# Attention in a hybrid layer: large probability tiles scaled in two halves, and rope and VectorE's query units one tile step later

## The chip, the core and the metric

The kernel runs on one core of a Trainium2 chip. The metric is device time in microseconds of one execution; lower is better. The core has five engines with queues of their own: TensorE (PE, with its weight loads shown apart as PEld), VectorE (DVE), ScalarE (ACT), GpSimd (POOL) and SyncE (SP), which issues the transfers. Each engine runs its instructions strictly in the order in which they were written, and engines meet only at semaphores: `wait_ge` holds an engine's queue until a counter has reached a value.

## The reference, cut to what matters

The program is one decoder layer: half a SwiGLU feed-forward block, a token mixer of two branches (latent attention and a gated recurrence), and another half feed-forward block. The change touches the attention alone, 206 of 2229 us:

```python
q = (_rmsnorm(c_q, q_norm_g) @ w_uq).reshape(b, s, MLA_HEADS, QK_NOPE + QK_ROPE)
kv = (_rmsnorm(c_kv, kv_norm_g) @ w_ukv).reshape(b, s, MLA_HEADS, QK_NOPE + V_HEAD)
...
q_rope = _apply_rope(q_rope, cos[:, :, None, :], sin[:, :, None, :])
...
sc = jnp.einsum('bqhd,bkhd->bhqk', qn, k_nope) + jnp.einsum('bqhr,bkr->bhqk', qr, k_rope)
sc = jnp.where(causal[None, None], sc * scale, -jnp.inf)
p = jax.nn.softmax(sc, axis=-1).astype(v.dtype)
return jnp.einsum('bhqk,bkhd->bqhd', p, v)
```

There are 1024 positions, 8 heads, and per head 64 plain and 32 rotary dimensions for queries and keys and 64 for values, all in float32.

## The kernel before

**Numbers.** Every float32 operand of a product is split into a high and a low part; a product of two split operands is three matmuls (lines 88 to 90). ScalarE writes the high part (line 94) and VectorE the low part (line 98), so each operand passes ACT and then DVE.

**Tiles.** Attention goes through 64 tiles, n = 8h + s: head h, block s of 128 queries. A tile of block s sees s + 1 blocks of 128 keys, so it has 128 to 1024 columns. Tiles with s of 4 and above have more than 512 columns, and two pieces (b = 0, the first 512 columns, and b = 1, the rest); smaller tiles have one. Below, a head with even number is E, with odd number O, and "O4" is its tile of block 4.

**Path of one tile.** PE computes the scores (`scores`, L88 to L90 with tiles a_k and a_q, closed by the mask matmul L2245). DVE takes the negated row maximum (L2256). ACT takes the exponential with the row sum (`exponent`, L2266). POOL raises the sum to the power -1 (L2272) and scales the probabilities by it (L2275). PE transposes each block of 128 columns (`turn`, L2290) into PSUM banks 4 (piece 0) and 5 (piece 1). ACT and DVE split the transposed pieces (`turned_hi`, `turned_lo`, tile a_pt, L94 and L98). Twice per head PE multiplies them with the values (`product`, L2322), and ACT and DVE take the output (a_o, L2338 and L2343).

**Steps.** Each engine runs a function of its own for each step n, in this order (the step's function names are in the code below):

- PE: [product at s = 3 and 7], scores of n, transposes of n - 2, [the projection of a unit].
- DVE: [output], maximum of n, low parts of n - 2, [low part of rope], [low part of a pair of heads], [unit].
- ACT: [output], high parts of n - 2, [rope], exponential of n, [unit].
- POOL: [rope], normalisation of n.

**Units.** The queries and keys of the next head are projected in between, in units of 512 positions: a unit is 9 matmuls on PE for a query half ("q") and 6 for a key half ("k", for two heads at once). `beside(n)` says which unit runs beside tile n: in even heads q half 0 at s = 1 and q half 1 at s = 7; in odd heads k half 0 at s = 1, q half 0 at s = 3, k half 1 at s = 6, q half 1 at s = 7. The last head has none, so 14 query units run beside tiles. All write PSUM bank 7, so PE's next unit waits until DVE has done with the one before (`u_dve`). For a query unit ACT copies the plain rows (L2163), and DVE multiplies the rotary rows by sine and cosine (L2188, L2189, into the single buffers a_rot and a_rot2) and writes the low part of the plain rows (L2191). "Rope" is what follows: POOL adds the two products (L2207), ACT writes the high part (L2175), DVE the low part (L2216).

**Waits around the change.** `turn` of tile n needs tile n's scaled probabilities (`norm_done`) and, since the banks are shared, the low parts of the same piece of tile n - 1 (`pt_split`). `scores` of n needs the exponential of n - 2 (`p_done`).

Of the kernel before, what the change touches and what calls it, by code (L numbers as in the profile page):

```python
# [19 lines left out]
ALU = mybir.AluOpType  # L20
# [3 lines left out]
P = 128  # L24
# [4 lines left out]
HALF = 512  # L29
# [34 lines left out]
class Core:  # L64


    def __init__(self, nc, ctx):
        self.nc, self.ctx = nc, ctx
        self.ps = ctx.enter_context(nc.psum_tensor("ps", [P, 8, HALF], F32))
        self.squared = None  # L70
# [30 lines left out]
def half_of(hf):  # L101
    return slice(hf * HALF, (hf + 1) * HALF)
# [134 lines left out]
class TileNorm:  # L237
# [118 lines left out]
    def turn(self, pe, t, b, bank_free=None):  # L356
        pe.wait_ge(self.S["gained_r"], self.pres + t + 1)
        if bank_free is not None:
            pe.wait_ge(self.S["u_split"], self.split_count(bank_free))
        for k in range(DK):  # L360
            last = pe.transpose(self.c.ps[:, b + k // 4, (k % 4) * P:(k % 4 + 1) * P],  # L361
                                self.work(t)[:, k * P:(k + 1) * P], self.c.ident[:, :])
        last.then_inc(self.S["turned"], 1)
# [1612 lines left out]
HEAD_TILES = NT  # L1976
# [3 lines left out]
class Attention:  # L1980
# [6 lines left out]
    def __init__(self, c, w, lat, w_uq, w_ukv):  # L1987
        self.c, self.nc, self.w, self.lat = c, c.nc, w, lat
        names = ("v_done", "v_hi", "v_lo", "zero", "kr_hi", "kr_split", "kr_copied", "unit_done", "q_hi", "q_rot", "q_sum", "rope_hi", "q_split",
                 "k_hi", "u_dve", "s_done", "max_done", "p_done", "norm_done", "t_done", "pt_hi", "pt_split", "o_done",  # L1990
                 "o_aux", "o_add", "o_hi", "o_split")
        self.S = {n: c.sem("a_" + n) for n in names}
        vq = w_uq.rearrange("(k p) (h e) -> p k h e", p=P, h=HEADS)
        vkv = w_ukv.rearrange("(k p) (h e) -> p k h e", p=P, h=HEADS)
        self.n_v = w.new(KC * HEADS * VH)
        for k in range(KC):
            w.piece(self.n_v, w.raw_of(self.n_v)[:, k * HALF:(k + 1) * HALF].rearrange("p (h e) -> p h e", e=VH),
                    vkv[:, k, :, NOPE:NOPE + VH])
        self.n_a = []
        half = ROPE // 2  # L2000
        for h in range(HEADS):
            n = w.new(QC * P + (0 if h % 2 else KC * P))
            q = w.raw_of(n)[:, 0:QC * P].rearrange("p (k f) -> p k f", f=P)
            even = ((0, QK, 0), (QK, half, NOPE + half), (QK + half, half, NOPE))
            odd = ((0, half, NOPE + half), (half, half, NOPE), (ROPE, ROPE, NOPE), (NOPE, NOPE, 0))
            for to, width, at in odd if h % 2 else even:
                w.piece(n, q[:, :, to:to + width], vq[:, :, h, at:at + width])
            if h % 2 == 0:
                for k in range(KC):
                    w.piece(n, w.raw_of(n)[:, (QC + k) * P:(QC + k + 1) * P].rearrange("p (h e) -> p h e", e=NOPE),  # L2010
                            vkv[:, k, h:h + 2, 0:NOPE])
            self.n_a.append(n)
        u = AT_U
        self.pt_hi, self.pt_lo = (c.at(u + 16384 * i, f"a_pt{i}", [P, 8, 4, P], F32R) for i in range(2))
        self.q_hi, self.q_lo = ([c.at(u + 32768 + 4096 * (2 * par + i), f"a_q{par}{i}", [P, SEQ], F32R) for par in range(2)]
                                for i in range(2))
        k_at = (u + 49152, u + 57344, AT_AREA + 73728)
        self.k_hi, self.k_lo = ([c.at(at + 4096 * i, f"a_k{n}{i}", [P, SEQ], F32R) for n, at in enumerate(k_at)] for i in range(2))
        self.v = c.at(AT_AREA + 40960, "a_v", [P, HEADS, NT, P], F32R)
        self.rot, self.rot2 = c.at(AT_AREA + 81920, "a_rot", [P, HALF]), c.at(AT_AREA + 100352, "a_rot2", [P, HALF])  # L2020
        self.probs = c.at(AT_AREA + 83968, "a_probs", [P, 3, SEQ])
        self.o = c.at(AT_AREA + 96256, "a_o", [P, SEQ])
        self.o_lo3 = c.at(AT_AREA + 36864, "a_o_lo3", [P, SEQ], F32R)
        self.neg, self.rs, self.inv = (c.at(BASE + 2400 + 64 * i, f"a_s{i}", [P, 16]) for i in range(3))
        self.scale = float(QK) ** -0.5

        self.units = [("q", 0, 0), ("k", 0, 0), ("q", 0, 1), ("k", 0, 1)]
        for h in range(HEADS - 1):
            if h % 2:
                self.units += [("k", (h + 1) // 2, 0), ("q", h + 1, 0), ("k", (h + 1) // 2, 1), ("q", h + 1, 1)]  # L2030
            else:
                self.units += [("q", h + 1, 0), ("q", h + 1, 1)]
        self.index = {unit: i for i, unit in enumerate(self.units)}
        self.closes = [self.index[("k", 0, 1)]] + [self.index[("q", h, 1)] for h in range(1, HEADS)]
# [234 lines left out]
    def normalise(self, pool, n):  # L2269
        i = n % 16  # L2270
        pool.wait_ge(self.S["p_done"], n + 1)
        self.nc.gpsimd.tensor_tensor(self.inv[:, i:i + 1], self.rs[:, i:i + 1], self.c.expo[:, 1:2], ALU.pow)\  # L2272
            .then_inc(self.S["norm_done"], 1)
        pool.wait_ge(self.S["norm_done"], 2 * n + 1)
        self.nc.gpsimd.tensor_scalar(self.prob(n), self.prob(n), self.inv[:, i:i + 1], 1.0, ALU.mult, ALU.mult)\  # L2275
            .then_inc(self.S["norm_done"], 1)

    def turn(self, pe, n):
        c, s = self.c, n % HEAD_TILES
        pe.wait_ge(self.S["norm_done"], 2 * n + 2)  # L2280
        if n == 0:
            pe.wait_ge(self.S["u_dve"], 4)
        for b in self.pieces(n):
            if b == 0 and n > 0:
                pe.wait_ge(self.S["pt_split"], self.piece(n - 1, 0) + 1)
            if b == 1 and n >= HEAD_TILES or b == 1 and s > 4:
                pe.wait_ge(self.S["pt_split"], self.piece(n - 1 if s > 4 else n - 5, 1) + 1)
            for j in range(4 * b, min(4 * b + 4, s + 1)):
                at = s - j if b else j
                last = pe.transpose(c.ps[:, 4 + b, at * P:(at + 1) * P], self.prob(n)[:, j * P:(j + 1) * P], c.ident[:, :])  # L2290
            last.then_inc(self.S["t_done"], 1)
# [69 lines left out]
    def act_step(self, act, n):  # L2361
        h, s = n // HEAD_TILES, n % HEAD_TILES
        if s == 7:
            self.take(act, h, 0)
        if s == 3 and h > 0:
            self.take(act, h - 1, 1)
        if n >= 2:
            self.turned_hi(act, n - 2)
        if s == 3 and h > 0 and h % 2 == 0:
            self.pair_hi(act, h // 2 - 1, slice(0, SEQ), 2 * h)  # L2370
        if n == HEADS * HEAD_TILES - 1:
            self.pair_hi(act, 3, half_of(0), 2 * HEADS - 1)
        if n < HEADS * HEAD_TILES:
            if n > 0 and self.beside(n - 1):
                self.rope_act(act, self.beside(n - 1))
            self.exponent(act, n)
            if self.beside(n):
                self.unit_act(act, self.beside(n))

    def dve_step(self, dve, n):  # L2380
        h, s = n // HEAD_TILES, n % HEAD_TILES
        if s == 7:
            self.add(dve, h, 0)
        if s == 3 and h > 0:
            self.add(dve, h - 1, 1)
        if n < HEADS * HEAD_TILES:
            self.maximum(dve, n)
        if n >= 2:
            self.turned_lo(dve, n - 2)
        if n < HEADS * HEAD_TILES:  # L2390
            if n > 0 and self.beside(n - 1):
                self.rope_dve(dve, self.beside(n - 1))
            if s == 3 and h > 0 and h % 2 == 0:
                self.pair_lo(dve, h // 2 - 1, slice(0, SEQ), h // 2)
            if n == HEADS * HEAD_TILES - 1:
                self.pair_lo(dve, 3, half_of(0), 4)
            if self.beside(n):
                self.unit_dve(dve, self.beside(n))

    def pool_step(self, pool, n):  # L2400
        if n > 0 and self.beside(n - 1):
            pool.wait_ge(self.S["norm_done"], 2 * n)
            self.rope_pool(pool, self.beside(n - 1))
        self.normalise(pool, n)

    def pe_step(self, pe, n):
        h, s = n // HEAD_TILES, n % HEAD_TILES
# [237 lines left out]
def hybrid_layer(nc, a, out):  # L2645
# [6 lines left out]
    with ExitStack() as ctx:  # L2652
# [47 lines left out]
        with nc.Block() as block:  # L2700
# [530 lines left out]
            def _(pe):  # L3231
# [8 lines left out]
                for q in range(NT):  # L3240
                    turn(f1, q)
# [123 lines left out]
```

## Time and profile before

| what | us |
|---|---|
| median of 3 runs (2231.65 to 2235.87) | 2233.1 |
| the profiled execution, its own time | 2231.14 |
| span of its profile | 2229.3 |
| attention's tile steps in the profile | about 1237 to 1443 |
| one pair of heads within them (1304.44 to 1355.20) | 50.76 |

The span is the time between the first and last recorded instruction. In the profile's rows, start times are microseconds from the span's start; a bracket gives the idle time of the engine ahead of an instruction and the instruction that released it. Matmuls are pipelined, so the busy times of successive ones overlap.

### The profile page before, as it was taken

What the parts mean: (1) busy time and instruction counts of PE and PEld (TensorE: products, weight loads), DVE (VectorE), ACT (ScalarE), POOL (GpSimd) and SP (SyncE); (2) the same over time, 40 slices, a digit from 0 to 9 for tenths busy, and PEclk for the clock granted to TensorE, in tenths of its full rate; (3) what the DMA queues carried; (4) which work ended last, traced back from release to release, by engine and by line L of the source; (5) the groups of instructions that cost most, each with busy time, mean ns of one, the idle gap of its engine ahead of it and who ended that gap; (6) DMA issues with size and microseconds to landing.
All of it is one profiled execution on the core that took longest, in us unless ns stands there. A gap on an engine that the chain in (4) does not pass through costs nothing.

```text
span 2229.3 us, 25934 instructions
## 1 busy us (share of the span) xinstructions
PE 2145.4 (96%) x9837; PEld 1780.6 (80%) x9837; DVE 1367.7 (61%) x1719; ACT 979.3 (44%) x1559; POOL 405.3 (18%) x444
## 2 busy tenths in 40 slices
PE   5999999999999999999999888899899999999998
PEld 4888788878887888888888677788788888888886
DVE  7667865557587656211212788677856766557666
ACT  6443333334364776311323666545533333333444
POOL 3123320000032221000011455402213331000012
PEclk9999999999999999999999999999999999999999
DMA  3355442253442111222410100265335453216234
GB/s 123 95 171 186 159 166 71 68 196 102 153 161 84 52 52 50 76 67 66 134 43 25 29 10 10 104 218 194 108 103 190 165 193 119 71 51 228 94 137 156
DMA packets 220293, 249.85 MB, mean 112 GB/s; under 512 B 24261, under 2 KB 161546, under 8 KB 220170
## 3 DMA queue, kind: packets, MB, share of 16 engines
q1 hardware_dynamic: 220170, 248.19, 34.0%
q8 instruction: 79, 1.29, 0.2%
q14 instruction: 44, 0.36, 0.0%
HBM read 192.06 MB, written 55.57 MB: 111 GB/s over the span
## 4 chain that ended last, share of the span: by engine, by line
PE 86%; DVE 6%; ACT 3%; issue 2%; POOL 2%; DMA 0%; SPq 0%; POOLq 0%; ACTq 0%; DVEq 0%
PE ps L88 28%; PE ps L90 28%; PE ps L89 28%; PE ps L2322 1%; PE ps L2290 1%; ACT a_probs L2266 1%; POOL a_rot L2207 1%; DVE a_pt L98 1%; PE ps L361 0%; DVE a_s L2256 0%; DVE w_lo L98 0%; DVE entry_y L346 0%; DVE exit_x L1337 0%; DMA entry_x<-in_x_dram 0%; DVE ff_w_lo L98 0%
## 5 line engine op out<-in xcount | busy, mean ns | idle before, releaser
L98 DVE TENSOR_TENSOR ff_w_lo<-ff_raw,ff_w_hi 128x512 fp32r<-128x512 f32 x264 | 214.0, 814 | 171.8 <-ACT ff_w_hi L94 171.5
L88 PE MATMUL ps<-ff_t,ff_w_hi 128*128 128x512 f32 x704 | 274.1, 389 | 0.4 <-DVE ff_w_lo L98 0.2
L90 PE MATMUL ps<-ff_t,ff_w_lo 128*128 128x512 f32 x704 | 273.9, 389 | 0.0
L89 PE MATMUL ps<-ff_t,ff_w_hi 128*128 128x512 f32 x704 | 273.9, 389 | 0.0
L94 ACT ACTIVATE ff_w_hi<-ff_raw 128x512 fp32r<-128x512 f32 x264 | 164.9, 627 | 179.5 <-PE ps L90 173.0
L88 PE MATMUL ps<-d_b_hi,d_a_hi 128*128 128x512 f32 x608 | 237.5, 391 | 3.8 <-DVE d_a_lo L98 3.7
L90 PE MATMUL ps<-d_b_hi,d_a_lo 128*128 128x512 f32 x608 | 236.6, 389 | 0.0
L89 PE MATMUL ps<-d_b_lo,d_a_hi 128*128 128x512 f32 x608 | 236.6, 389 | 0.0
L98 DVE TENSOR_TENSOR w_lo<-w_raw,w_hi 128x1024 fp32r<-128x1024 f32 (+2 forms) x81 | 90.5, 1119 | 233.2 <-ACT w_hi L94 233.2
L88 PE MATMUL ps<-ff_b,ff_w_hi 128*128 128x512 f32 x528 | 208.0, 394 | 6.0 <-ACT ff_u2x L696 5.0
L89 PE MATMUL ps<-ff_b,ff_w_hi 128*128 128x512 f32 x528 | 206.8, 392 | 0.0
L90 PE MATMUL ps<-ff_b,ff_w_lo 128*128 128x512 f32 x528 | 206.7, 391 | 0.0
L88 PE MATMUL ps<-u_hi,w_hi 128*128 128x512 f32 x512 | 199.7, 390 | 0.0
L90 PE MATMUL ps<-u_hi,w_lo 128*128 128x512 f32 x512 | 199.4, 389 | 0.0
L89 PE MATMUL ps<-u_lo,w_hi 128*128 128x512 f32 x512 | 199.3, 389 | 0.0
L88 PEld LDWEIGHTS ps<-ff_t,ff_w_hi 128*128 128x128 f32 x704 | 132.1, 188 | 28.7 <-DVE ff_w_lo L98 0.6
L89 PEld LDWEIGHTS ps<-ff_t,ff_w_hi 128*128 128x128 f32 x704 | 132.1, 188 | 27.5
L90 PEld LDWEIGHTS ps<-ff_t,ff_w_lo 128*128 128x128 f32 x704 | 132.1, 188 | 27.3
L94 ACT ACTIVATE w_hi<-w_raw 128x1024 fp32r<-128x1024 f32 (+2 forms) x81 | 78.3, 968 | 151.7 <-PE ps L90 145.2
L88 PEld LDWEIGHTS ps<-d_b_hi,d_a_hi 128*128 128x128 f32 x608 | 114.1, 188 | 29.5 <-DVE d_a_lo L98 6.1
L90 PEld LDWEIGHTS ps<-d_b_hi,d_a_lo 128*128 128x128 f32 x608 | 114.1, 188 | 23.6
L89 PEld LDWEIGHTS ps<-d_b_lo,d_a_hi 128*128 128x128 f32 x608 | 114.2, 188 | 23.5
(301 smaller groups left out, 4297.6 us busy)
## 6 DMA issues: line engine op xcount, KB each, us to landing
ff_raw<-in_ffn_w_gate_dram SPq DMA_DIRECT2D x44, 512.0 KB, 3.9
ff_raw<-in_ffn_w_up_dram SPq DMA_DIRECT2D x44, 512.0 KB, 4.0
d_sums<-in_ffn_w_down_dram SPq DMA_DIRECT2D x44, 512.0 KB, 4.1
sums_scratch<-d_sums SPq DMA_DIRECT2D x88, 256.0 KB, 2.6
w_raw<-in_w_in_dram SPq DMA_DIRECT2D x32, 512.0 KB, 4.0
d_raw<-sums_scratch SPq DMA_DIRECT2D x24, 512.0 KB, 3.3
w_raw<-in_w_out_dram SPq DMA_DIRECT2D x24, 512.0 KB, 4.2
spill_scratch<-ff_st SPq DMA_DIRECT2D x44, 256.0 KB, 2.9
```

Of the source, the lines that this page charges most:

```text
L88: pe.matmul(out, lh, rh, start=start, stop=False, skip_group_check=go_on)
L89: pe.matmul(out, lh, rl, start=False, stop=False, skip_group_check=go_on)
L90: return pe.matmul(out, ll, rh, start=False, stop=stop, skip_group_check=go_on)
L94: return nc.scalar.activation(hi, src, ACT.Copy)
L98: return nc.vector.tensor_tensor(lo, src, as_f32(hi), ALU.subtract)
L2207: self.nc.gpsimd.tensor_tensor(self.rot[rope, :], self.rot[rope, :], self.rot2[rope, :], ALU.add)\
L2266: self.nc.scalar.activation(self.prob(n), self.seen(n), ACT.Exp, bias=self.neg[:, i:i + 1], scale=1.0, accum_out=self.rs[:, i:i + 1]).then ...
L2290: last = pe.transpose(c.ps[:, 4 + b, at * P:(at + 1) * P], self.prob(n)[:, j * P:(j + 1) * P], c.ident[:, :])
L2322: last = pe.matmul(c.ps[:, 6, first * P:HALF], self.v[:, h, j, :], pt[:, unit, first:4, :].rearrange("p b q -> p (b q)"), start=j + i == 0 ...
```

## The change

Three things change, all within the tile steps.

1. `normalise` scales a tile of more than 512 columns by one instruction per piece, and each adds one to `norm_done`; the power has a semaphore of its own (`inv_done`). `turn` waits for `norm_done` piece by piece.
2. On DVE, a query unit beside tile n moves from the end of step n to the end of step n + 1. Key units stay. The rope's steps on ACT and DVE move from step n + 1 to n + 2.
3. On POOL, the rope addition of the unit beside n stays in step n + 1, but comes behind tile n + 1's normalisation.

PE's order is the same in both.

```diff
     def normalise(self, pool, n):
...
         self.nc.gpsimd.tensor_tensor(self.inv[:, i:i + 1], self.rs[:, i:i + 1], self.c.expo[:, 1:2], ALU.pow)\
-            .then_inc(self.S["norm_done"], 1)
-        pool.wait_ge(self.S["norm_done"], 2 * n + 1)
-        self.nc.gpsimd.tensor_scalar(self.prob(n), self.prob(n), self.inv[:, i:i + 1], 1.0, ALU.mult, ALU.mult)\
-            .then_inc(self.S["norm_done"], 1)
+            .then_inc(self.S["inv_done"], 1)
+        pool.wait_ge(self.S["inv_done"], n + 1)
+        for b in self.pieces(n):
+            part = self.prob(n)[:, b * HALF:min((b + 1) * HALF, (n % HEAD_TILES + 1) * P)]
+            self.nc.gpsimd.tensor_scalar(part, part, self.inv[:, i:i + 1], 1.0, ALU.mult, ALU.mult).then_inc(self.S["norm_done"], 1)
 
     def turn(self, pe, n):
         c, s = self.c, n % HEAD_TILES
-        pe.wait_ge(self.S["norm_done"], 2 * n + 2)
         if n == 0:
             pe.wait_ge(self.S["u_dve"], 4)
         for b in self.pieces(n):
+            pe.wait_ge(self.S["norm_done"], self.piece(n, b) + 1)
...
     def act_step(self, act, n):
...
-            if n > 0 and self.beside(n - 1):
-                self.rope_act(act, self.beside(n - 1))
+            if n > 1 and self.beside(n - 2):
+                self.rope_act(act, self.beside(n - 2))
             self.exponent(act, n)
...
     def dve_step(self, dve, n):
...
-            if n > 0 and self.beside(n - 1):
-                self.rope_dve(dve, self.beside(n - 1))
+            if n > 1 and self.beside(n - 2):
+                self.rope_dve(dve, self.beside(n - 2))
...
-            if self.beside(n):
+            before = self.beside(n - 1) if n > 0 else None
+            if before and before[0] == "q":
+                self.unit_dve(dve, before)
+            if self.beside(n) and self.beside(n)[0] == "k":
                 self.unit_dve(dve, self.beside(n))
 
     def pool_step(self, pool, n):
+        self.normalise(pool, n)
         if n > 0 and self.beside(n - 1):
-            pool.wait_ge(self.S["norm_done"], 2 * n)
+            pool.wait_ge(self.S["norm_done"], self.piece(n, len(self.pieces(n)) - 1) + 1)
             self.rope_pool(pool, self.beside(n - 1))
-        self.normalise(pool, n)
```

The order on DVE at the passage from an even to an odd head (tiles E7, O0, O1), before, from the low parts of E5 on:

```order
L98 TENSOR_TENSOR a_pt_165<-ps,a_pt_164 128x2x128
L2188 TENSOR_TENSOR a_rot_178<-ps,trig 32x512
L2189 TENSOR_TENSOR a_rot<-ps,trig 32x512
L2191 SCALAR_TENSOR_TENSOR a_q_169<-ps,a_q_167 64x512
L2256 TENSOR_REDUCE a_s_182<-ps 128x1
L98 TENSOR_TENSOR a_pt_165<-ps,a_pt_164 128x4x128
L98 TENSOR_TENSOR a_pt_165<-ps,a_pt_164 128x3x128
L2216 SCALAR_TENSOR_TENSOR a_q_169<-a_rot,a_q_167 32x512
L2256 TENSOR_REDUCE a_s_182<-ps 128x1
L98 TENSOR_TENSOR a_pt_165<-ps,a_pt_164 128x4x128 x2
```

and the same place in the changed kernel:

```order
L98 TENSOR_TENSOR a_pt_165<-ps,a_pt_164 128x2x128
L2256 TENSOR_REDUCE a_s_182<-ps 128x1
L98 TENSOR_TENSOR a_pt_165<-ps,a_pt_164 128x4x128
L98 TENSOR_TENSOR a_pt_165<-ps,a_pt_164 128x3x128
L2188 TENSOR_TENSOR a_rot_178<-ps,trig 32x512
L2189 TENSOR_TENSOR a_rot<-ps,trig 32x512
L2191 SCALAR_TENSOR_TENSOR a_q_169<-ps,a_q_167 64x512
L2256 TENSOR_REDUCE a_s_182<-ps 128x1
L98 TENSOR_TENSOR a_pt_165<-ps,a_pt_164 128x4x128 x2
L2216 SCALAR_TENSOR_TENSOR a_q_169<-a_rot,a_q_167 32x512
```

The unit's three instructions moved behind the maximum of O0 and the low parts of E6, and the rope's low part (L2216) behind the maximum of O1 and the low parts of E7.

The order on POOL from tile O4 to O5, before; the first row is the rope of the query unit beside O3:

```order
L2207 TENSOR_TENSOR a_rot<-a_rot,a_rot_178 32x512
L2272 TENSOR_TENSOR a_s_184<-a_s_183,expo 128x1
L2275 TENSOR_SCALAR a_probs<-a_probs,a_s_184 128x640
L2272 TENSOR_TENSOR a_s_184<-a_s_183,expo 128x1
L2275 TENSOR_SCALAR a_probs<-a_probs,a_s_184 128x768
```

and in the changed kernel:

```order
L2272 TENSOR_TENSOR a_s_184<-a_s_183,expo 128x1
L2277 TENSOR_SCALAR a_probs<-a_probs,a_s_184 128x512
L2277 TENSOR_SCALAR a_probs<-a_probs,a_s_184 128x128
L2207 TENSOR_TENSOR a_rot<-a_rot,a_rot_178 32x512
L2272 TENSOR_TENSOR a_s_184<-a_s_183,expo 128x1
L2277 TENSOR_SCALAR a_probs<-a_probs,a_s_184 128x512
L2277 TENSOR_SCALAR a_probs<-a_probs,a_s_184 128x256
```

The rope's addition moved behind the power and the scaling of O4, and each scaling became two instructions.

## Rows read from the trace of the kernel before

**Rows 1.** The page: busy time of each engine.

```profile
PE 2145.4 (96%) x9837; PEld 1780.6 (80%) x9837; DVE 1367.7 (61%) x1719; ACT 979.3 (44%) x1559; POOL 405.3 (18%) x444
```

**Rows 2.** Windows: length, then busy us of PE, PEld, DVE, ACT, POOL; granted clock.

```profile
1236.00:1442.00 206.00, 177.48 (x998) 147.00 (x997) 162.95 (x258) 135.36 (x294) 104.36 (x142) 0.96 0.13 42
1304.44:1355.20 50.76, 43.84 (x259) 36.44 (x258) 42.59 (x68) 34.83 (x76) 26.87 (x36) 1.00 0.04 11
...
1297.50:1300.90 3.40, 3.40 (x15) 2.99 (x15) 2.67 (x4) 1.78 (x5) 2.19 (x4) 0.50 0.01 2
```

**Rows 3.** Waits in 1236 to 1442: us in total, times, longest us.

```profile
PE ps L2290 <- DVE a_pt L98: 22.5, 20, 1.8
ACT a_q L2175 <- POOL a_rot L2207: 19.9, 14, 1.9
...
PEld ps L2290 <- POOL a_probs L2275: 2.7, 8, 0.7
```

**Rows 4.** Timeline of PE, 1308 to 1340: start us, us, instruction, [idle before].

```profile
1308.95 0.23 PE L2245 MATMUL ps<-mask_b,ident_b 128*128 128x128 bf16 x1
...
1312.17 1.06 PE L2290 MATMUL ps<-ident,a_probs 128*128 128x128 f32 x8 [1.80 <-DVE a_pt L98]
1312.99 0.48 PE L88 MATMUL ps<-ckv,w_hi 128*128 128x512 f32 x1
...
1322.40 0.23 PE L2245 MATMUL ps<-mask_b,ident_b 128*128 128x128 bf16 x1
...
1325.10 0.63 PE L2290 MATMUL ps<-ident,a_probs 128*128 128x128 f32 x4 [1.01 <-DVE a_pt L98]
...
1332.98 0.47 PE L88 MATMUL ps<-cq,w_hi 128*128 128x512 f32 x1
...
1339.23 0.47 PE L88 MATMUL ps<-cq,w_hi 128*128 128x512 f32 x1
```

**Rows 5.** Timeline of DVE, 1308 to 1332.

```profile
1308.87 0.68 DVE L2188 TENSOR_TENSOR a_rot<-ps,trig 32x512 f32<-32x512 f32 x1 [0.41 <-PE ps L90]
...
1311.02 0.29 DVE L2256 TENSOR_REDUCE a_s<-ps 128x1 f32<-128x128 f32 x1
1311.34 1.16 DVE L98 TENSOR_TENSOR a_pt<-ps,a_pt 128x512 fp32r<-128x512 f32 x2
...
1321.63 0.69 DVE L2188 TENSOR_TENSOR a_rot<-ps,trig 32x512 f32<-32x512 f32 x1 [0.57 <-PE ps L90]
...
1325.88 0.96 DVE L2256 TENSOR_REDUCE a_s<-ps 128x1 f32<-128x768 f32 x1
...
1330.70 1.39 DVE L98 TENSOR_TENSOR a_k<-ps,a_k 64x512 fp32r<-64x512 f32 x2 [0.81 <-ACT a_k L94]
```

**Rows 6.** Timeline of ACT, 1309 to 1331.

```profile
1309.66 0.98 ACT L94 ACTIVATE a_pt<-ps 128x512 fp32r<-128x512 f32 x2 [0.20 <-PE ps L2290]
...
1323.00 0.49 ACT L94 ACTIVATE a_pt<-ps 128x384 fp32r<-128x384 f32 x1 [0.77 <-PE ps L2290]
1324.51 0.62 ACT L2175 ACTIVATE a_q<-a_rot 32x512 fp32r<-32x512 f32 x1 [1.02 <-POOL a_rot L2207]
...
1326.87 0.90 ACT L2266 ACTIVATE a_probs<-ps,a_s 128x768 f32<-128x768 f32 x1 [0.34 <-DVE a_s L2256]
```

**Rows 7.** Timeline of POOL, 1308 to 1325.

```profile
1308.85 0.55 POOL L2272 TENSOR_TENSOR a_s<-a_s,expo 128x1 f32<-128x1 f32 x1 [2.04 <-ACT a_probs L2266]
...
1318.85 1.15 POOL L2275 TENSOR_SCALAR a_probs<-a_probs,a_s 128x384 f32<-128x384 f32 x1
...
1323.20 1.28 POOL L2207 TENSOR_TENSOR a_rot<-a_rot,a_rot 32x512 f32<-32x512 f32 x1 [0.23 <-DVE a_rot L2189]
```

**Rows 8.** Groups by shape in 1236 to 1442: busy us, mean ns | idle.

```profile
L2275 POOL TENSOR_SCALAR a_probs<-a_probs,a_s 128x1024 f32<-128x1024 f32 x8 | 9.0, 1124 | 0.8
...
L2275 POOL TENSOR_SCALAR a_probs<-a_probs,a_s 128x512 f32<-128x512 f32 x8 | 5.6, 696 | 0.8
...
L2275 POOL TENSOR_SCALAR a_probs<-a_probs,a_s 128x128 f32<-128x128 f32 x8 | 3.0, 376 | 0.8
```

More of the change, by code:

```diff
@@ L1989, in __init__ @@
         names = ("v_done", "v_hi", "v_lo", "zero", "kr_hi", "kr_split", "kr_copied", "unit_done", "q_hi", "q_rot", "q_sum", "rope_hi", "q_split",
-                 "k_hi", "u_dve", "s_done", "max_done", "p_done", "norm_done", "t_done", "pt_hi", "pt_split", "o_done",
+                 "k_hi", "u_dve", "s_done", "max_done", "p_done", "inv_done", "norm_done", "t_done", "pt_hi", "pt_split", "o_done",
                  "o_aux", "o_add", "o_hi", "o_split")
```

## The prediction, on record before the run

> **What bounds the kernel now.** The page's busy times come first: PE is busy for 2145 of 2229 us [rows 1], so what stands outside attention (matmul on matmul) cannot be touched by this change, which moves nothing there. The windows come next: in attention's 206 us PE is busy for 177.5, so 28.5 us of pauses are all that a better order could win. A pair of heads takes 50.76 us, with PE pausing for 6.9 and DVE for 8.2 [rows 2]. The waits say for what: 22.5 us go to transposes that wait for DVE's low parts of the tile before (`pt_split`), and only 2.7 to transposes that wait for POOL's scaling [rows 3]. So the bound is a chain that passes through PE and DVE in turn: maximum, low parts and units stand in one queue on DVE, and PE waits for some of them. The timeline then shows where: 1.80 us ahead of E7's transposes and 1.01 ahead of O3's [rows 4]. In both places a query unit stands on DVE ahead of the low parts waited for.
>
> **Part 1, scaling in halves.** A scaling has a fixed part: 0.376 us for 128 columns, 0.696 for 512, 1.124 for 1024 [rows 8]. Two halves of 512 take 1.39, so the first is ready 0.43 earlier and the second 0.27 later, and the 32 large tiles cost POOL 32 x 0.27 = 8.6 us more, in a queue that is idle half of the time (104 busy of 206 [rows 2]). What PE can gain is at most the 2.7 us of rows 3, and the part of that which belongs to small tiles stays. I take 0 to -1, and 0 in the sum, because the second half is later, and what is behind it on POOL (the rope, part 3) too.
>
> **Part 2, the query unit on DVE a step later.** A unit is 2.15 us on DVE (1308.87 to 1311.02 [rows 5]). Before, it ran while DVE had nothing else: scores and high parts of the next step were not there yet. Now it stands behind them. I walk through the places with the rows' durations.
>
> *Place A, from an even to an odd head.* PE's unit q1 is done at 1308.87, when DVE starts. The scores of O0 end at 1308.95 + 0.23 = 1309.2 [rows 4], so DVE now waits, does the maximum in 0.3 until 1309.5, and waits again: ACT's high part of E6 starts at 1309.66 and its first piece takes some 0.6 of the 0.98 for both [rows 6]. The low parts take 0.7 and 0.5, until 1311.5 (1.16 for both [rows 5]). E7's transposes can start at 1311.1 instead of 1312.17, a gain of 1.0. But then comes the unit, 1311.5 to 1313.6, and PE's next unit (k half 0) overwrites the bank that it reads. It started at 1312.99 [rows 4] and now starts at about 1313.75: **+0.8**. The pause was moved, not removed, and it grew.
>
> *Place B, tiles O3 to O7.* DVE is free at 1321.63 - 0.57 = 1321.06 [rows 5] and now waits for the scores of O4, until 1322.40 + 0.23 = 1322.6 [rows 4]. The maximum is 0.83 (between 0.29 for one block and 0.96 for six [rows 5]), until 1323.45; the high part of O2 ends at 1323.49 [rows 6], its low part at 1324.0. O3's transposes gain the 1.0 of rows 4. The unit follows until 1326.15, its two rotary products until 1325.45; the maximum of O5 until 1327.1 (before: 1325.88 + 0.96 = 1326.84) and the low part of O3 until 1327.8.
>
> **Part 3, the rope.** In the waits ACT stood 19.9 us for POOL's rope addition [rows 3]; it stood ahead of an exponential. It still does, one tile later. On POOL the addition is now behind O4's normalisation: exponential of O4 from 1323.5 to 1324.4, power 0.55 [rows 7], halves 0.70 and 0.38 [rows 8], with the gaps until 1326.35; the addition 1.28 [rows 7] until 1327.65; ACT's part 0.62 [rows 6] until 1328.3. The exponential of O5 started at 1326.87 [rows 6] and now starts 1.4 later. DVE's low part of rope ends at 1329.0, the maximum of O6 (1.1) at 1330.1. Before, 1326.84 + 0.7 + 1.1 gives 1328.7. The exponential of O6 and the key copies behind it on ACT slip with it, so DVE's key unit moves from 1330.70 [rows 5] to about 1331.9, and PE's q1, which waits for it, from 1332.98 [rows 4] to 1333.45: +0.45.
>
> *Place C, from an odd to an even head.* DVE has the key unit (1.4), the output (0.6), the maximum of O7 (1.2) and the low parts of O5 (1.0) until 1336.15; then the maximum of the next tile. ACT does O7's exponential and the query copy until 1336.9 and the first high piece of O6 until 1337.5. Low parts until 1338.7, unit until 1340.85, PE's next unit at 1341.0 instead of 1339.23 [rows 4]: **+1.8**, with B's 0.45 in it.
>
> *Place D, tiles E1 to E4.* The query unit moves behind the maximum of E2, in a stretch where DVE waited for the rope and for a weight's high part; the rope's low part now stands ahead of the pair's low part. By my walk 0 to +0.3; I take 0.
>
> **Sum.** A pair costs 0.8 + 1.8 = 2.6 by the walk, 2.9 with D. Counted by DVE's pauses instead: 1.5 for 0.41 at A, 1.3 + 0.5 for 0.57 at B, which is 2.3. I take 2.4. There are three pairs (from head 0's E7 to head 6's): 7.2. At the last passage, to head 7, no unit follows on PE, and only the product waits: +0.4. Together **+7.6 us**. The profiled execution took 2231.14, which gives 2238.7; the median of the runs is 2.0 higher, so I predict 2240.7. What is 0.2% or less (4.5 us) would hardly be told from no change.
>
> **The clock, and a collision.** The granted clock was 0.50 (1.2 GHz) at 1297.5 to 1300.9, just behind a pause of PE; in the whole pair from 1304.44 on, with all its pauses, it stayed at 1.00 [rows 2]. New pauses at A and C are longer in sum than the old (0.8 + 1.5 where 1.8 was), so more such dips may come, at most 1.7 us each and mostly less, since part of a dip lies in waits. By the Trainium skill, "TensorE: Matmul & The Clock Gate", Part 1, the clock is halved after idling and given back after sustained work; this would speak against the change, and these rows agree in kind.
>
> A scaling of 384 columns took 1.15 us at 1318.85 [rows 7], as long as one of 1024, while DVE was on a weight's low part, which reads two SBUF operands. The rope's low part is such an instruction too, and there are 32 more scalings for it to meet. By the Trainium skill, "SBUF — State Buffer", Who interferes with whom, the two engines lock a shared pair of ports for a whole instruction; the row agrees. I price neither in the sum; together they are the upper end, 14 query units x 0.5 = 7 us more.
>
> **Rivals.**
>
> *Faster: the transposes' pauses vanish.* If PE's unit does not come to wait for DVE, because the 1.0 gained at A, B and C is kept (the turns are earlier, so high and low parts are), the 10 places give 10 x 1.0, so -10: 2223. For it speaks that 22.5 of 28.5 us of pauses are just this wait [rows 3]. Against it: bank 7. It decides where the low parts of E6 plus 2.15 end ahead of E7's transposes; they take 1.06 [rows 4], so the unit is 1.1 too late plus the second piece. Chance 0.16.
>
> *Same: moved pauses only.* DVE pauses for 8.2 us in a pair [rows 2]; if the delays at A to C fall into pauses further on (O5 to O7 and E2 to E5), each place gives back what it took: 2233, within 4. Against it: between O3 and O6 DVE has nearly none. This takes in the case that the moved part does nothing. Chance 0.18.
>
> *Slower by more: dips and collisions.* As above: 2248 and more. Chance 0.08.
>
> *The forecast.* +4.5 to +14. Chance 0.58.
>
> **Range.** 2230 to 2248: it leaves out the faster rival (0.16) and the far end of the slow one. The likeliest case's own range is 2237 to 2247. Slower by over 0.2%: 0.66; within: 0.18; faster: 0.16.
>
> **What would show it.** In the changed trace the transposes' wait for a_pt at E7 (1.80) shrinks below 1.0, and a new wait of PE appears ahead of the first matmul of the unit beside s = 1, for DVE's a_q (L2191), of 1 to 2 us, six times. ACT's wait for the rope stays above 12 us, now ahead of O5. DVE gets pauses ahead of the maximum of O4. A pair of heads takes about 53.2 us. I am wrong if PE's unit at s = 1 does not wait, or if a pair takes less than 50.8.

## The result, and the profile after

The changed kernel takes 2249.18 us (median of 4 runs, 2248.58 to 2250.03) against 2232.38 before (4 runs, 2230.67 to 2235.87): ratio 1.0074, 95% interval 1.0056 to 1.0091, or 16.8 us slower. Slower was forecast, but by 7.6 us, and 2249 lies above the range's end of 2248, where its rival "slower by more" stood (chance 0.08). A few executions in the study were far slower than others of the same kernel (one took 4179.92 us); the ratios leave them out.

The page of the changed kernel, its span and busy times, beside [rows 1]:

```profile
span 2247.2 us, 25997 instructions
...
PE 2154.9 (96%) x9837; PEld 1787.3 (80%) x9837; DVE 1370.9 (61%) x1719; ACT 979.0 (44%) x1559; POOL 413.6 (18%) x476
```

The span is 17.9 us longer than before. Its windows are next, with columns as in [rows 2] (the last two are the DMA's busy share and its GB/s): six heads (from the transposes of tile 7 of head 0 to those of tile 7 of head 6), one pair of heads, and two short stretches.

```profile
1259.34:1430.72 171.38, 143.59 (x768) 118.24 (x769) 130.30 (x202) 104.34 (x225) 88.10 (x133) 0.92 0.04 11
1315.15:1372.83 57.68, 48.30 (x256) 39.70 (x257) 43.42 (x68) 34.84 (x75) 29.44 (x45) 0.91 0.03 10
1300.50:1307.30 6.80, 6.20 (x25) 5.11 (x24) 4.54 (x6) 2.77 (x6) 5.07 (x8) 0.52 0.00 0
1317.60:1321.00 3.40, 3.28 (x9) 2.69 (x9) 2.41 (x5) 1.65 (x4) 1.91 (x3) 0.53 0.02 5
```

The same six heads in the kernel before:

```profile
1260.74:1414.60 153.86, 133.82 (x769) 111.81 (x769) 127.98 (x202) 104.50 (x226) 80.62 (x108) 0.98 0.05 16
```

Nearly all is here: 171.38 us for 153.86. The pair takes 57.68 where [rows 2] has 50.76. The new fact stands in the column of the granted clock: 0.91 over the pair, where it was 1.00, and the two short stretches at about half, the second in the pair and the first ahead of it. A stretch like the first stands in the pair too, from 1358.7 to 1365.7. PE's busy time grows with it, from 43.8 to 48.3 us, with the same instructions.

The waits in 1236 to 1460, beside [rows 3]:

```profile
PE ps L2291 <- DVE a_pt L98: 22.1, 21, 2.1
...
ACT a_q L2175 <- POOL a_rot L2207: 17.6, 11, 2.1
...
DVE a_s L2256 <- PE ps L2245: 17.5, 19, 1.9
...
ACT a_probs L2266 <- DVE a_s L2256: 16.4, 21, 1.6
...
PEld ps L2291 <- POOL a_probs L2277: 9.8, 12, 1.2
...
PE ps L88 <- issue: 8.9, 6, 1.5
```

The transposes still wait 22.1 us for the low parts (22.5 before). The waits that are new or grew are VectorE's maximum for the scores, the exponential for the maximum, the transposes' weight loads for the scaled probabilities (9.8 us where [rows 3] has 2.7; it is 3.1 in e1's trace and 9.1 in e2's, so it comes with the delays and not with the halves), and the last row, 8.9 us in 6 times: this is the unit beside block 1, which the timeline of PE shows:

```profile
1261.91 0.47 PE L88 MATMUL ps<-ckv,w_hi 128*128 128x512 f32 x1 [1.48 <-issue]
...
1282.04 0.47 PE L88 MATMUL ps<-cq,w_hi 128*128 128x512 f32 x1
...
1289.45 0.47 PE L88 MATMUL ps<-cq,w_hi 128*128 128x512 f32 x1 [1.49 <-issue]
...
1310.52 0.47 PE L88 MATMUL ps<-cq,w_hi 128*128 128x512 f32 x1
...
1315.15 1.09 PE L2291 MATMUL ps<-ident,a_probs 128*128 128x128 f32 x8 [0.75 <-DVE a_pt L98]
...
1317.72 0.65 PE L88 MATMUL ps<-ckv,w_hi 128*128 128x512 f32 x1 [1.48 <-issue]
```

Transposes of eight blocks (tile 7) now pause for 0.75 us instead of 1.80, and the unit behind them for 1.48, where before it ran on at once [rows 4]. The profile calls this wait "issue", since its releaser was not matched; it ends 0.10 us after VectorE's L2191 at 1317.6, so I read it as the wait for the unit before. For the comparison, these are the starts of the query units before (the others are in [rows 4]):

```profile
1306.53 0.48 PE L88 MATMUL ps<-cq,w_hi 128*128 128x512 f32 x1
...
1357.29 0.48 PE L88 MATMUL ps<-cq,w_hi 128*128 128x512 f32 x1
```

From one start to the next the four places of the prediction can be measured.

| place | from, to | before | changed | difference |
|---|---|---|---|---|
| A | q1 beside E7, k0 beside O1 | 6.46 | 7.20 | +0.74 |
| B | k0, q1 beside O7 | 19.99 | 20.13 | +0.14 |
| C | q1, q0 beside E1 | 6.25 | 7.41 | +1.16 |
| D | q0, q1 beside E7 | 18.05 | 21.07 | +3.02 |

A, B and C were read where the clock was at 1.00. D has the stretch of 6.8 us at half clock in it.

VectorE, in B at O4 and at the rope beside O5, in C at the low parts of O6, and in D at the rope of E1:

```profile
1271.48 0.82 DVE L2256 TENSOR_REDUCE a_s<-ps 128x1 f32<-128x640 f32 x1 [1.46 <-PE ps L2245]
...
1277.02 0.68 DVE L2216 SCALAR_TENSOR_TENSOR a_q<-a_rot,a_q 32x512 fp32r<-32x512 f32 x1 [0.51 <-ACT a_q L2175]
...
1286.03 1.16 DVE L98 TENSOR_TENSOR a_pt<-ps,a_pt 128x512 fp32r<-128x512 f32 x2 [0.98 <-ACT a_pt L94]
...
1299.25 0.68 DVE L2216 SCALAR_TENSOR_TENSOR a_q<-a_rot,a_q 32x512 fp32r<-32x512 f32 x1 [0.60 <-ACT a_q L2175]
```

It now waits 1.46 us for the scores of O4 ahead of the maximum (forecast 1.3), 0.98 for ACT's high part of O6, and 0.51 and 0.60 for ACT's rope parts. The rope at O5, on POOL and on ACT:

```profile
1273.95 1.04 POOL L2277 TENSOR_SCALAR a_probs<-a_probs,a_s 128x512 f32<-128x512 f32 x2
...
1275.08 1.26 POOL L2207 TENSOR_TENSOR a_rot<-a_rot,a_rot 32x512 f32<-32x512 f32 x1
```

```profile
1276.37 0.63 ACT L2175 ACTIVATE a_q<-a_rot 32x512 fp32r<-32x512 f32 x1 [2.06 <-POOL a_rot L2207]
```

As forecast the addition comes right behind the two halves of O4, and ACT waits for it, 2.06 us.

### The profile page after: what moved, and what is told of

Read it like the earlier page. It is cut to its first block, busy times and chain, and to the rows that moved or that the text cites. A ratio compares the mean times of both kernels' runs of the same rounds, so it can differ in the third digit from the quotient of the medians.

```text
span 2247.2 us, 25997 instructions
## 1 busy us (share of the span) xinstructions
PE 2154.9 (96%) x9837; PEld 1787.3 (80%) x9837; DVE 1370.9 (61%) x1719; ACT 979.0 (44%) x1559; POOL 413.6 (18%) x476
## 4 chain that ended last, share of the span: by engine, by line
PE 88%; DVE 6%; ACT 2%; issue 2%; POOL 1%; DMA 0%; SPq 0%; POOLq 0%; ACTq 0%; DVEq 0%
PE ps L88 28%; PE ps L90 28%; PE ps L89 28%; PE ps L2291 1%; PE ps L2323 1%; DVE a_s L2256 1%; PE ps L361 1%; DVE w_lo L98 1%; DVE a_pt L98 0%; ACT a_probs L2266 0%; DVE entry_y L346 0%; DVE exit_x L1337 0%; DMA entry_x<-in_x_dram 0%; DVE d_a_lo L98 0%; ACT a_pt L94 0%
```

## The experiments

All times are medians, and ratios are to the kernel before on the same chip. The experiments ran on four chips, on which the kernel before had medians of 2232.34 to 2233.45, so a difference in us between two runs is good to about 1 us. Where an edit names places, E and O are even and odd heads and the number is the block.

### The parts apart

**e1_halves**: the change without its delays.

```diff
+    def late(self, n):
+        return bool(self.beside(n)) and self.beside(n)[0] == "q" and n % HEAD_TILES in ()
+
+    def soon(self, n):
+        return bool(self.beside(n)) and not self.late(n)
...
+            if n > 0 and self.late(n - 1):
+                self.unit_dve(dve, self.beside(n - 1))
+            if self.soon(n):
                 self.unit_dve(dve, self.beside(n))
```

The rope on ACT, DVE and POOL follows the same test, in the step before or after.

> The scaling in two halves alone: units and rope stand as in the kernel before. Theory (the order on VectorE and the clock make the whole loss): the halves change nothing that can be told, ratio 0.9985 to 1.0005, since before only 2.7 us of waits were for a scaling. Rival (the 32 more instructions on GpSimd, or their meeting with VectorE on SBUF, cost something): 1.001 or more, with more than 3 us of waits for a_probs from GpSimd.

Measured: 2233.41 us, ratio 1.0004 (0.9995 to 1.0012). The halves alone change nothing that the times can tell. The trace is finer: a pair of heads at full clock takes 51.20 us, 0.43 above the 50.77 of the same window before (1312.17 to 1362.94).

```profile
1312.84:1364.04 51.20, 43.98 (x256) 36.42 (x257) 42.59 (x68) 34.72 (x75) 28.68 (x45) 1.00 0.04 11
```

**e2_later**: the delays with each tile scaled by one instruction, as before.

> The delay of query units and rope alone: each tile is scaled by one instruction. Theory: the loss is nearly all here, ratio to the kernel before 1.006 to 1.009, and a pair of heads takes 56 to 58 us. Rival (the halves carry part of it, by delaying the rope's addition by some 0.3 us and the second piece of each large tile): 1.005 or less.

Measured: 2246.32 us, ratio 1.0059 (1.0046 to 1.0072). The ratio is just below the range that I had for it, and the pair takes 57.59 us (expected 56 to 58): the delays carry nearly all of the loss. The 2.9 us between this and the changed kernel are no more than the two intervals allow; e14 and e15 come back to it.

**e3_not_s1**: delays only beside blocks 3 and 7, `n % HEAD_TILES in (3, 7)`.

> The changed kernel, with the query units beside block 1 of even heads as in the kernel before; those beside blocks 3 and 7 stay delayed. Order theory: the stretch from the unit beside E1 to the scores of the next head's first tile, 20.2 us before and 23.2 after, goes back to below 21; four units fewer are late; the ratio falls to 1.003 to 1.005. Clock theory: the stretch of 6.8 us at half clock behind E2 comes from the pauses around E1 and E2 as a whole; if it stays, so do about 2 us of the 3 per pair, and the ratio is 1.005 to 1.007.

Measured: 2242.85 us, ratio 1.0045 (1.0031 to 1.0059). The time fell as the order theory said, but it did not leave the clock alone: the six heads have 17 us at half clock, where the changed kernel has 27. So this run did not tell the two theories apart.

### The clock

**e4_filled**: matmuls that nobody needs, in PE's pauses.

```diff
+    def fill(self, pe, n, count):
+        h, s = n // HEAD_TILES, n % HEAD_TILES
+        rows, k = slice(0, P if h % 2 else QK), self.k_of(h)
+        if count:
+            pe.wait_ge(self.S["o_add"], 2 * h if s > 3 else 2 * h - 1)
+        for i in range(count):
+            pe.matmul(self.c.ps[:, 6, :], self.q_hi[h % 2][rows, s * P:(s + 1) * P], self.k_hi[k][rows, 0:HALF], start=True, stop=True)
+
     def pe_step(self, pe, n):
...
         self.scores(pe, n)
+        if h > 0:
+            self.fill(pe, n, {(0, 1): 3, (1, 1): 3, (0, 4): 4, (0, 5): 2, (1, 6): 7}.get((h % 2, s), 0))
         if n >= 2:
             self.turn(pe, n - 2)
+        if h > 0 and self.beside(n):
+            self.fill(pe, n, {(0, 1): 6, (1, 1): 6}.get((h % 2, s), 0))
```

> The changed kernel, with TensorE's pauses of heads 1 to 7 filled by matmuls of 512 columns whose result nobody reads (bank 6, overwritten by the next product): 3 ahead of E7's and O7's transposes, 6 ahead of the unit beside block 1, 4 and 2 ahead of the transposes in steps E4 and E5, 7 in O6. The result is unchanged. Clock theory: with the pauses filled the granted clock stays at 1.00 in attention except at its start, where it fell to 0.50 for 10.2 us per pair, and the time falls by 5 to 10 us, ratio to the kernel before 1.003 to 1.006. Order theory (the pauses themselves are the loss, the clock changes nothing on the way that sets the end): the same time or up to 4 us more, 1.007 to 1.010, whatever the clock does.

Measured: 2240.47 us, ratio 1.0035 (1.0023 to 1.0048). With more work the kernel is 8.7 us faster. The profiled execution was the slowest of its five (2243.92). Its windows, of the six heads and of a pair:

```profile
1259.77:1422.69 162.92, 157.02 (x863) 125.34 (x862) 129.87 (x202) 104.31 (x225) 88.28 (x133) 0.99 0.05 12
1313.66:1367.55 53.89, 51.87 (x288) 41.41 (x288) 43.29 (x68) 34.74 (x75) 29.52 (x45) 1.00 0.04 11
```

The granted clock is back at 1.00 in the pair, and the pair takes 53.89 us. This is the price of the order alone (the halves' part with it): 3.1 us above the 50.76 before. The fillings themselves do not add to it: A, B and C together take 34.76 us here and 34.74 in the changed kernel, both at full clock. The place D, without its dip:

```profile
1343.82 0.47 PE L88 MATMUL ps<-cq,w_hi 128*128 128x512 f32 x1
...
1362.95 0.48 PE L88 MATMUL ps<-cq,w_hi 128*128 128x512 f32 x1
```

19.13 us, so D costs 1.08 at full clock, and the rest of its 3.02 was the clock.

**e10_before_fill**: the control, the kernel before with fillings in its own pauses (heads 1 to 6: 5 at block 1, 5 in E4, 3 in O5).

> Control: the kernel before with fill matmuls in its own pauses in heads 1 to 6 (5 ahead of tile 7's transposes, 5 in E4, 3 in O5), nothing else. Theory (filling acts only through the clock): the two stretches of 3.4 us at half clock in heads 2 and 6 go, which cost 0.7 and 0.9 us; ratio 0.9990 to 0.9998. Rival (filling helps or hurts in itself): more than 2 us either way.

Measured: 2230.28 us, ratio 0.9990 (0.9982 to 0.9999).

```profile
1261.42:1414.16 152.74, 143.68 (x817) 117.07 (x818) 127.74 (x202) 104.56 (x226) 80.58 (x108) 1.00 0.06 16
1312.28:1363.09 50.81, 48.27 (x274) 39.30 (x275) 42.58 (x68) 34.83 (x76) 26.85 (x36) 1.00 0.04 12
```

The pair is unchanged (50.81), so here the filling does nothing in itself. The six heads gained 1.1 us, and the two stretches of 3.4 us that they had at half clock are gone.

**e5_fill_E45** and **e6_fill_s1**: the filling of e4 at one place each, `{(0, 4): 4, (0, 5): 2}` ahead of the transposes, and `{(0, 1): 3, (1, 1): 3, (1, 6): 7}` with the 6 ahead of the unit.

> The changed kernel with fill matmuls only ahead of the transposes in steps E4 and E5 (4 and 2, even heads). Theory (each half-clock stretch follows the pauses just ahead of it): the stretches of 6.8 us behind E2's late low parts go, those of 3.4 us behind the unit beside O1 stay; some 1.5 to 2 us per pair come back, ratio to the kernel before 1.004 to 1.006. Rival (the clock looks at the pair as a whole, or the gain of the full filling came from elsewhere): both kinds of stretches stay, ratio above 1.0065.

> The changed kernel with fill matmuls only in the steps of block 1 (3 ahead of the transposes, 6 ahead of the unit) and 7 in O6. Theory: the 3.4 us stretches behind O1 go, those of 6.8 us at E3 and E4 stay; about 1 to 1.5 us per pair that had one come back, ratio 1.005 to 1.007. Rival as for the run with E4 and E5 filled: the place of the filling makes no difference, both lose or keep all stretches.

Measured: 2242.99 us, ratio 1.0042 (1.0030 to 1.0055), and 2246.45 us, ratio 1.0062 (1.0049 to 1.0075). A pair in the first, and in the second:

```profile
1313.13:1366.96 53.83, 45.87 (x263) 37.35 (x263) 43.29 (x68) 34.75 (x75) 29.46 (x45) 1.00 0.04 11
```

```profile
1315.12:1370.18 55.06, 51.59 (x281) 41.66 (x282) 43.30 (x68) 34.73 (x75) 29.49 (x45) 0.97 0.04 11
```

Six matmuls per pair ahead of two transposes give back 6.2 us of 8.7 (7.1 by the ratios). The theory held in the main for where the clock falls. In the second run the stretches behind O1 went, and of the three of 6.8 us in E3 to E5 two stayed and one shrank to 3.4. In the first run all three of 6.8 us went. Of the two behind the unit beside O1, in heads 3 and 5, one went, although nothing was filled at O1, and one stayed:

```profile
1369.00:1372.40 3.40, 2.87 (x7) 2.32 (x8) 2.82 (x5) 1.19 (x3) 1.93 (x2) 0.51 0.02 5
```

### The order

**e7_rope_ahead**: all fillings in heads 1 to 6, and in step 3 ACT's rope part ahead of the pair's high part.

```diff
+        if s == 3 and n > 1 and self.beside(n - 2):
+            self.rope_act(act, self.beside(n - 2))
         if s == 3 and h > 0 and h % 2 == 0:
             self.pair_hi(act, h // 2 - 1, slice(0, SEQ), 2 * h)
...
-            if n > 1 and self.beside(n - 2):
+            if s != 3 and n > 1 and self.beside(n - 2):
                 self.rope_act(act, self.beside(n - 2))
```

> The changed kernel with all fillings (in heads 1 to 6 only, so the last head is as changed), and with ScalarE's rope part in step E3 ahead of the high part of a pair of heads instead of behind it. Theory: at full clock a pair costs 3.1 us more than before, of which 1.1 between the unit beside E1 and the next query unit, because rope's low part waits 0.6 us for ScalarE and holds back the pair's low part and the maximum of E4; this order gives back 0.4 to 0.7 us of it, so that the stretch from the unit beside E1 to the next unit, 19.2 us, becomes 18.5 to 18.8; time 2236 to 2239. Rival (that 1.1 is the price of the output and the filling, not of rope's place): the stretch stays at 19.2.

Measured: 2239.50 us, ratio 1.0031 (1.0020 to 1.0043). The total is 0.5 us above what I expected, but the pair and the stretch D are as the theory has them:

```profile
1313.15:1366.40 53.25, 51.79 (x288) 41.36 (x288) 43.28 (x68) 34.69 (x75) 29.57 (x45) 1.00 0.04 11
```

```profile
1343.28 0.47 PE L88 MATMUL ps<-cq,w_hi 128*128 128x512 f32 x1
...
1361.80 0.48 PE L88 MATMUL ps<-cq,w_hi 128*128 128x512 f32 x1
```

18.52 us for D: 0.6 of its 1.1 were the place of one rope instruction, ahead of which a copy of 1.06 us waits for the output.

**e11_late3**: only the three query units beside O3 delayed, scalings whole.

> The kernel before with the delay of unit and rope for the three query units beside O3 alone, scalings whole. Theory from the segments of the changed kernel (20.1 us from the unit beside O1 to that beside O7, 20.0 before): within 0 to +0.3 us each, ratio 0.9998 to 1.0008, though TensorE's pause moves from O3 (1.0) to O4 (1.7). Rival (my forecast for this place, +0.45 and 1.4 us late on VectorE, which the next passage pays): 1.0010 or more.

Measured: 2238.97 us, ratio 1.0030 (1.0019 to 1.0042). Three moved units cost 6.6 us, where I expected under 2. A pair, from the transposes of O7 in head 1 on:

```profile
1288.02:1343.33 55.31, 47.86 (x257) 40.12 (x257) 42.71 (x68) 34.69 (x75) 26.81 (x37) 0.91 0.04 11
```

Here too the clock is at 0.91. This is the worst of the three pairs; the six heads have 17 us at half clock.

**e13_late3_fill**: the same with fillings in heads 1 to 6 (5 in E1, 3 in O1, 5 in E4, 7 in O6).

> The kernel of the run with only O3's units delayed (2239.0), with fill matmuls in heads 1 to 6: 5 ahead of E7's transposes and 3 ahead of O7's, 5 in E4, 7 in O6. Theory (what the delay of three units costs by order is 0.5 to 1.0 us each, the rest of the 6.6 is the clock): granted clock 1.00 from head 1 on, a pair in 51.5 to 52, 2232 to 2235. Rival (it is the order, and more of it than I read from the segments): 2237 or more, a pair in 52.5 or more.

Measured: 2233.44 us, ratio 1.0006 (0.9998 to 1.0015). The pair:

```profile
1312.04:1363.67 51.63, 48.56 (x277) 39.68 (x277) 42.59 (x68) 34.74 (x76) 26.81 (x36) 1.00 0.04 11
```

51.63 us at full clock, 0.9 above before, which is 2.6 for three pairs. The filling gave back 5.5 us here and 2.1 in the control. So of the 6.6 us some 3 to 4 were the clock.

**e12_rope_first_pool**: the changed kernel with the rope's addition ahead of the normalisation on POOL.

> The changed kernel with GpSimd's order as before: the rope's addition ahead of the next tile's normalisation, both in step n + 1, everything else as changed. Theory (the addition behind the normalisation makes ScalarE's rope part late at O5 by 0.3 to 1 us only, and ahead of it it would hold back a normalisation until VectorE's delayed products are there, 2 us or more): slower than the changed kernel by 2 to 10 us, ratio 1.008 to 1.012. Rival (my forecast: the addition's place behind the normalisation is what makes O5 late, 1.4 us): faster than the changed kernel by 1 us or more, ratio 1.007 or less.

Measured: 2260.24 us, ratio 1.0120 (1.0105 to 1.0136). Its waits:

```profile
POOL a_rot L2207 <- DVE a_rot L2189: 37.1, 14, 3.6
...
PEld ps L2291 <- POOL a_probs L2277: 26.6, 20, 2.9
```

POOL stands 37.1 us for VectorE's delayed products, and what is behind it, the normalisation, is missed by PE. Part of the loss is the clock again: the trace has 48 us at half clock between 1260 and 1440, where the changed kernel has 27. In this kernel, once the unit is late, the addition is better behind the normalisation.

### Do the halves add to the delays?

**e14_later_fill** and **e15_changed_fill**: e2's kernel and the changed one, both with e5's fillings, in heads 1 to 6.

> The delay alone, scalings whole, with fill matmuls in E4 (4) and E5 (2), heads 1 to 6. It had 2246.3 without them. Theory (at full clock the halves neither cost nor give): a pair in 53.6 to 54.1 like the changed kernel with the same filling, ratio of the two within 0.1%, 2239 to 2243. Rival (halves cost in the changed kernel, whose time was 3 us above this one's without filling): 2 us or more below the next kernel.

> The changed kernel with the same filling, 4 in E4 and 2 in E5, in heads 1 to 6 and none in the last head. Theory: a pair in 53.8 as measured with the filling in all heads, and the last head 1 us faster than there: 2240 to 2242. Rival as for the run before: slower than it by 2 us or more.

Measured on one chip: 2241.49 us, ratio 1.0043 (1.0029 to 1.0056), and ratio 1.0045 (1.0032 to 1.0059) with a median of 2244.12, from few and scattered runs (four between 2238.88 and 2244.44). The times show no cost of the halves; one of up to some 3 us beside the delays is not excluded by them. The pairs at full clock are finer: 53.59 us in e14, against 53.83 in e5, so the halves cost 0.24 a pair beside the delays and 0.43 alone (e1).

```profile
1312.76:1366.35 53.59, 45.63 (x262) 37.29 (x263) 43.36 (x68) 34.73 (x75) 27.55 (x37) 1.00 0.04 11
```

e15 is a second measurement of e5, not a new kernel. The filling of e5 stands in even heads only, and the last head is odd, so both issue the same instructions; my expectation that they differ in the last head was wrong. The comparison is worth having all the same, since the half-clock stretches lie elsewhere. e15 has one in head 2, at 1291.9 to 1295.4, which e5 lacks, and one behind O1's unit of head 3:

```profile
1319.20:1322.60 3.40, 3.19 (x8) 2.67 (x9) 2.50 (x5) 1.45 (x4) 1.91 (x3) 0.51 0.02 5
```

In e5 that place was at full clock, and the stretch stood in head 5. So the place of a single stretch of 3.4 us in one trace says little.

### Something faster?

**e8_split_unit**: the kernel before, with one of the unit's three instructions (L2191) behind the next maximum and low parts.

```diff
     def dve_step(self, dve, n):
...
+            if self.split(n - 1):
+                self.low_dve(dve, self.beside(n - 1))
             if n > 0 and self.beside(n - 1):
                 self.rope_dve(dve, self.beside(n - 1))
...
-                self.unit_dve(dve, self.beside(n))
+                self.unit_dve(dve, self.beside(n), not self.split(n))
```

> The kernel before, with only one of a query unit's three VectorE instructions moved a step later: the low part of the plain rows (L2191) goes behind the next tile's maximum and the low parts, the two rotary products stay. Scalings whole, rope in its old step. Theory (the products fill a pause of VectorE and must stay; the low part stood in the transposes' way): the transposes of tile 7 start 0.7 us earlier, the unit behind them 0.3 earlier, 0.6 to 1.4 us per pair, ratio 0.9980 to 0.9995. Rival (anything of the unit behind the low parts costs as much as it gives, since the next unit waits for it): 1.0000 to 1.0015.

Measured: 2233.32 us, ratio 1.0001 (0.9992 to 1.0010). PE at the passage to head 3's O1 and at O6's scores:

```profile
1310.84 1.06 PE L2299 MATMUL ps<-ident,a_probs 128*128 128x128 f32 x8 [1.08 <-DVE a_pt L98]
...
1311.98 0.47 PE L88 MATMUL ps<-ckv,w_hi 128*128 128x512 f32 x1
...
1325.51 0.50 PE L88 MATMUL ps<-a_k,a_q 128*128 128x512 f32 x1 [0.83 <-ACT a_probs L2275]
```

The pause ahead of E7's transposes fell from 1.80 to 1.08 and the unit comes 0.4 us earlier, but there is a wait of 0.83 at O6, which was 0.36 before. The six heads of this trace have 17 us at half clock, the kernel before 7, so this run alone does not say what the order is worth.

**e9_split_halves_fill**: that with the scalings in halves and fillings in heads 1 to 6 (4 at block 1, 5 in E4, 2 in O5).

> The kernel before with the split query unit of the run before (only the low part of the plain rows a step later), the scalings in halves and fill matmuls in heads 1 to 6 (4 ahead of the transposes of tile 7, 5 in E4, 2 in O5). Theory: the split unit gives 0.4 to 0.5 us at each passage to an odd or even head at full clock, which the half-clock stretches of 6.8 us took back; with the pauses filled they stay away, and in halves the first piece no longer waits for GpSimd. 2228 to 2231, ratio 0.998 to 0.9995, a pair of heads in 50.0 us or less. Rival (the gain of the split unit is an effect of where the pauses lie, and the fillings delay as much as they save): 1.000 to 1.002.

Measured: 2233.93 us, ratio 1.0005 (0.9996 to 1.0013). The pair:

```profile
1311.48:1362.72 51.24, 48.64 (x271) 38.90 (x272) 42.76 (x68) 34.69 (x75) 28.75 (x45) 1.00 0.04 11
```

51.24 at full clock is 0.5 more than the whole unit in its old place (50.76), and about what the halves alone cost (51.20 in e1). Place by place, A and C gain 0.4 and 0.3, B loses 0.65 and D 0.5; how much of this the halves do is not separated. Both runs came out in the rival's range. The fastest kernel of the study is e10's, by 0.1%.

## Why the prediction was wrong, by its steps

**What bounds the kernel**: right. The loss is in the tile steps alone, 17.5 of 17.9 us in six heads.

**Part 1, halves: 0**: right within what the times can tell (e1, 1.0004). In the traces they cost 0.24 to 0.43 us a pair, so they took a little and gave nothing.

**Part 2, places A and C**: right in kind and nearly in size. The pause ahead of tile 7's transposes fell to 0.75, and the unit behind them waits 1.48, in all six places, as the last part of the prediction asked for; ACT's wait for the rope stayed, at 17.6 us. A cost 0.74 (forecast 0.8), B with C 1.30 (forecast 1.8): B was over-counted, 0.14 for 0.45.

**Part 3, the rope**: the walk was right (ACT's wait at O5 2.06, VectorE's 0.51 behind it), and its wording misleads: not the place behind the normalisation is at fault. e12 shows that the other place costs 10 to 11 us more.

**Place D: 0**: the first term that was mis-sized. At full clock it cost 1.08, 0.6 of it the rope part that stands behind the pair's high part (e4 against e7). I had seen that order and let my own 0 to 0.3 stand without pricing ACT's copy ahead of it.

**The sum**: 2.4 for a pair, 3.1 measured at full clock (e4 against [rows 2]), which is 9.3 for three pairs. By the fillings the six heads are 162.92 - 152.74 = 10.2 us longer; e4's have one stretch of 3.4 us at half clock, the control's none. I had 7.2. The last passage is on top, with 1.3 us in the last head for the forecast 0.4, and 1.4 us less ahead of head 0's E7.

**The clock**: this is the step that failed. "I price neither in the sum": the rest, 17.5 less 9.3 to 10.2, which is 7.3 to 8.2 us, came from it. The changed kernel spends 27 us of the six heads at half clock, the one before 7. I had the right rows and the right rival ("new pauses at A and C are longer in sum than the old") but took the clock for an upper end of 7 us that was shared with a collision and given a chance of 0.08. What I missed is a warning in the trace before: the same place was at 0.50 in heads 2 and 6 (1297.4 to 1301.0 and 1399.8 to 1403.4), and at 1.00 in head 4, within the pair of [rows 2]. From there small losses of order came with larger ones of the clock: e11 lost some 2.6 us by order in three pairs and 6.6 in all. The Trainium skill, "TensorE: Matmul & The Clock Gate", Part 1, has the clock fall behind idling. The runs agree in kind: with PE's pauses filled the granted clock of the six heads went from 0.92 to 0.99 (e4), and in the kernel before from 0.98 to 1.00 (e10).

**The collision** has no cost that shows: VectorE's busy time of a pair went from 42.6 to 43.4, and the halves alone cost at most the 0.43 us a pair of e1. No run tests the collision by itself.

**The rivals.** The faster one fell where the prediction said that it would: PE's unit had to wait. The one of moved pauses is right for B alone.

**Open**: which pause brings which half-clock stretch. Where the pauses in E4 and E5 were filled, the stretches of 6.8 us went in every trace (e4, e5, e7, e14, e15), and this much fits "the pause just ahead". The stretches of 3.4 us do not settle it: e5 and e15 are one program and have them in different heads. The split between order and clock does not hang on this.

## What to carry to other kernels

A unit that fills one engine's wait is not in the way of what stands behind it: ask what the engine would do in its place before moving it. When a change lets the matmul engine pause more, price the granted clock as a term of its own, from the stretches at either level in the trace, and above all where the trace before already shows one fall. Compare places at the same granted clock, too: two traces of one program can have a stretch in different heads. Filling its pauses with matmuls that nobody reads is a cheap test that splits a loss into order and clock, with the same filling in the kernel before as the control.

## What the runs showed of the hardware

- More matmuls made a kernel faster: 31 more in a pair of heads gave back 8.7 us in all (e4), 6 of them alone 6 to 7 (e5, e15).
- A us at half clock cost about a third of a us here: 171.38 - 162.92 = 8.5 us for some 24 us more at 0.50, since part of each stretch lies in waits. The difference is between the changed kernel and e4.
- The granted clock fell to 0.50 in stretches of 3.4 or 6.8 us although no pause of PE in the six heads of the changed kernel was longer than 1.7 us.
- One program had its half-clock stretches at different places in two executions (e5 and e15).
- GpSimd took 32 instructions more (444 to 476 in the pages) at a ratio of 1.0004 (e1); it was busy for 104 of attention's 206 us before [rows 2].
